# Recurrence levels of a hybrid encoder: keys of both directions in one stationary operand, one matmul per block in place of two

## The reference, cut to what matters

```python
log_f = jnp.logaddexp(jnp.log(lb), jnp.log1p(-lb) + jax.nn.log_sigmoid(z))
k = -jnp.expm1(log_f)
qd = jax.nn.silu(...) * (HG_DK ** -0.5)
...
cum = jnp.cumsum(gc, axis=2)
rel = jnp.where(mask[:, :, None], cum[:, :, :, None, :] - cum[:, :, None, :, :], -jnp.inf)
attn = jnp.einsum('nhtk,nhtsk,nhsk->nhts', qc, jnp.exp(rel), kc)
o = attn @ vc + jnp.einsum('nhtk,nhkv->nhtv', qc * jnp.exp(cum), state)
...
o = o[0] + jnp.flip(o[1], 1)
```

## Time and profile before

| | |
|---|---|
| median of 3 runs | 1437.44 us |
| lowest and highest run | 1436.44, 1437.8 us |
| span of the profiled execution | 1437.8 us |
| time of the profiled execution | 1437.8 us, the highest of the three runs |
| level matmuls, line 767 | 168 instructions, 336 records, from 429.1 us to 531.3 us |
| level 8, line 772 | last starts at 534.18 us |

### The profile page before, as it was taken

The page is one execution under the profiler, slowest core; times in us unless marked ns, Lnnn a source line. Parts: engine busy times, 40 slices in busy tenths (PEclk is TensorE's granted clock), DMA queues, the critical chain, the costliest instruction groups (busy, mean ns, idle before and its releaser), DMA issues.

```text
span 1437.8 us, 23522 instructions
## 1 busy us (share of the span) xinstructions
PE 1329.0 (92%) x9366; PEld 1238.5 (86%) x9366; DVE 1022.9 (71%) x1536; ACT 717.2 (50%) x1147; POOL 150.5 (10%) x122
## 2 busy tenths in 40 slices
PE   7599899999799999799999899899998999699997
PEld 6489799999689998799998798899997998699996
DVE  4186777677859867877778677777678565777677
ACT  4185365555462233555554633655554763555552
POOL 0000300000304430300002002100003001300001
PEclk8789999999999999999999899899998999899999
DMA  7454265555352233365553374455553543265551
GB/s 255 112 202 130 89 202 189 193 190 180 108 183 90 90 103 132 126 227 183 189 186 132 132 231 140 161 205 182 188 188 109 199 133 118 89 233 177 187 191 47
DMA packets 64019, 230.09 MB, mean 160 GB/s; under 512 B 7431, under 2 KB 9223, under 8 KB 62887
## 3 DMA queue, kind: packets, MB, share of 16 engines
q1 hardware_dynamic: 63910, 228.60, 47.6%
HBM read 225.95 MB, written 2.62 MB: 159 GB/s over the span
## 4 chain that ended last, share of the span: by engine, by line
PE 67%; issue 18%; DVE 6%; DMA 4%; POOL 2%; ACT 2%; SPq 0%; POOLq 0%; DVEq 0%; ACTq 0%
PE proj L572 14%; PE proj L573 13%; PE proj L574 13%; PE acc L599 5%; PE acc L601 5%; PE acc L600 5%; DMA raw<-in_stream 4%; PE side L767 2%; PE proj L584 1%; DVE y_tok L1154 1%; PE proj L586 1%; PE proj L588 1%; POOL rstd L1267 1%; DVE w_lo L976 1%; PE acc L668 1%
## 5 line engine op out<-in xcount | busy, mean ns | idle before, releaser
L572 PE MATMUL proj<-xT_hi,w_hi 128*128 128x256 f32 x2000 | 579.8, 290 | 37.5 <-issue 33.0
L976 DVE TENSOR_TENSOR w_lo<-raw,w_hi 128x1024 fp32r<-128x1024 f32 x404 | 480.7, 1220 | 170.2 <-ACT w_hi L784 168.4
L784 ACT ACTIVATE w_hi<-raw 128x1024 fp32r<-128x1024 f32 x404 | 427.1, 1060 | 318.7 <-PE proj L574 144.8
L573 PE MATMUL proj<-xT_lo,w_hi 128*128 128x256 f32 x2000 | 574.2, 287 | 0.0
L574 PE MATMUL proj<-xT_hi,w_lo 128*128 128x256 f32 x2000 | 573.8, 287 | 0.0
L572 PEld LDWEIGHTS proj<-xT_hi,w_hi 128*128 128x128 f32 x2000 | 393.0, 196 | 46.3 <-issue 44.9
L573 PEld LDWEIGHTS proj<-xT_lo,w_hi 128*128 128x128 f32 x2000 | 392.8, 196 | 1.5
L574 PEld LDWEIGHTS proj<-xT_hi,w_lo 128*128 128x128 f32 x2000 | 392.2, 196 | 0.0
L989 DVE SCALAR_TENSOR_TENSOR cv<-hid,fconv_w,cv 128x255 f32<-128x255 f32 x176 | 77.4, 481 | 139.5 <-ACT cv L824 139.5
L601 PE MATMUL acc<-w_hi,gT_lo 128*128 128x512 f32 x352 | 139.0, 395 | 0.0
L600 PE MATMUL acc<-w_lo,gT_hi 128*128 128x512 f32 x352 | 139.0, 395 | 0.0
(11 more groups left out here) (169 smaller groups left out, 1566.1 us busy)
## 6 DMA issues: line engine op xcount, KB each, us to landing
raw<-in_stream SPq DMA_DIRECT2D x404, 512.0 KB, 4.7
gains<-in_ln SPq DMA_DIRECT2D x8, 1024.0 KB, 8.5
bias<-bias_scratch SPq DMA_DIRECT2D x2, 1152.0 KB, 8.0
bias_scratch<-bias_rows SPq DMA_DIRECT2D x1, 1536.0 KB
x_tok<-in_x SPq DMA_DIRECT2D x2, 512.0 KB, 4.4
y_tok<-in_mem SPq DMA_DIRECT2D x1, 1024.0 KB, 10.1
out<-x_tok SPq DMA_DIRECT2D x2, 512.0 KB, 2.8
masks_in<-in_masks_c SPq DMA_DIRECT2D x1, 512.0 KB, 11.5
```

Of the source, the lines that this page charges most:

```text
L572: pe.matmul(bank, w_hi[:, slot, at], a_hi(k, every), start=(k == 0), stop=False)
L573: pe.matmul(bank, w_hi[:, slot, at], a_lo(k, every), start=False, stop=False)
L784: nc.scalar.activation(w_hi[:, u % SPLIT, :], raw[:, u % RAW, :], ACT.Copy).then_inc(hi_ready, 1)
L976: v.tensor_tensor(w_lo[:, u % SPLIT, :], raw[:, u % RAW, :], w_hi[:, u % SPLIT, :].bitcast(F32), ALU.subtract).then_inc(lo_ready, 1)
```

## The change

ScalarE gets a new item "keys" behind each level below 7. It copies, for a pair of heads, the forward keys of the first half and the backward keys of the second half of each double block of the next level, 512 columns, into a free part of the buffer `ex`. TensorE then uses that as the stationary operand and reads the queries crosswise: the first half of each double block from the backward queries, the second half from the forward ones, 128 columns in one matmul. For that `QD` and `KE` become the two halves of one tensor each. The copy waits for the same two grow semaphores as the level's matmuls, which wait for the copy as well.

```diff
@@ make_schedule
                 for n in range(LEVELS + 1):
                     at.setdefault(first + n, []).append(it("level", p, n))
+                    if n + 1 < LEVELS:
+                        at[first + n].append(it("keys", p, n + 1))
@@ trunk_kernel
-        QD = [sb(f"qd{d}", [P, HEADS, SEQ]) for d in range(2)]
-        KE = [sb(f"ke{d}", [P, HEADS, SEQ]) for d in range(2)]
+        qd = sb("qd", [P, 2, HEADS, SEQ])
+        ke = sb("ke", [P, 2, HEADS, SEQ])
+        QD = [qd[:, d] for d in range(2)]
+        KE = [ke[:, d] for d in range(2)]
...
+        def level_keys(p):
+
+            return ex[:].rearrange("p a b c s -> p (a b c s)")[:, p * 512:(p + 1) * 512]
+
+        def crossed(of, lower, p, start, count, b):
+
+
+            other = HEADS * SEQ
+            return bass.AP(tensor=of, offset=lower * other + 2 * p * SEQ + start,
+                           ap=[[2 * other, P], [2 * b, count // (2 * b)], [b + (1 - 2 * lower) * other, 2], [1, b]])
...
+        keys_ready = [sem(f"keys_ready{p}") for p in range(PAIRS)]
@@ tensor, item "level"
+                    if 1 <= n < LEVELS:
+                        pe.wait_ge(keys_ready[p], n)
...
                             elif n < LEVELS:
-
-                                for d in range(2):
-                                    dst = bank[:, col:col + P].rearrange("p (n two b) -> p n two b", two=2, b=b)
-                                    q = QD[d][:, h, keys].rearrange("p (n two b) -> p n two b", two=2, b=b)
-                                    last = pe.matmul(dst[:, :, 1 - d, :], KE[d][:, h, keys], q[:, :, 1 - d, :],
-                                                     start=True, stop=True)
+                                last = pe.matmul(bank[:, col:col + P].rearrange("p (n two b) -> p n two b", two=2, b=b),
+                                                 level_keys(p)[:, col:col + P], crossed(qd, 1, p, col, P, b),
+                                                 start=True, stop=True)
@@ scalar
+                elif name == "keys":
+                    p, n = item[2], item[3]
+                    b = 2 ** (n - 1)
+                    act.wait_ge(fw_ready[p], n)
+                    if n >= 2:
+                        act.wait_ge(bw_ready[p], n - 1)
+                    nc.scalar.activation(level_keys(p).rearrange("p (n two b) -> p n two b", two=2, b=b),
+                                         crossed(ke, 0, p, 0, 512, b), ACT.Copy).then_inc(keys_ready[p], 1)
```

## The result

The changed kernel takes **1445.86 us** (median of 5 runs, 1444.0 to 1446.2) against 1437.5 of the kernel before (5 runs, 1436.44 to 1438.23): ratio 1.0046, 95% interval 1.0031 to 1.0061. It is slower by half a per cent. The forecast was 1438.8, no change, with 1435.9 to 1441.5 as its own range, and the result lies outside that. Only the wider range of 1430 to 1447, which covers the rivals, holds it, and the direction is that of the slower ones.

The account below looks back on a forecast made before the run. TensorE was taken to bound the kernel, VectorE close behind. Schedule -1.6 us plus clock +3.0 gave +1.4 on the 1437.44 median: 1438.8 us, no change, own range 1435.9 to 1441.5, wider range 1430 to 1447.

Parts of the forecast that it names:

- the ring: Layer 1 recurrence levels: the cycle copy, w_hi, w_lo, post work, grow, copy; 5.4 us with FF/FB, 6.8 with HQ.
- Schedule: 105.1 becomes 103.5: Layer 1 recurrence levels, first to last weight load: step sums give 1.6 us won of 18.9.
- Steps with FF/FB post work: Levels 1 to 2 and 3 to 4: 5.50 and 4.84 us before, 5.4 each after.
- Steps without post work: Levels 2 to 3 and 4 to 5, set by GpSimd's chain: 4.85 and 4.65 us before, 4.7 and 4.5 after.
- HQ steps: Levels 5 to 6, with HQ post work on VectorE: 5.49 us before, 6.8 after, TensorE still for 3.1.
- step 7 to 8: Level 8 waits for two grows and two masked copies on VectorE: 7.81 to about 8.2 us; pair two 7.2 after.
- Pair three: Last head pair's levels, V and G chunks with little VectorE work: 26.82 us before, 23.9 after.
- The clock: Slow TensorE clock after four pauses over 2.15 us: 4 by 0.75 = 3.0 us lost, bounds 0 and 6.8.
- Rival 1: Faster: only the copy's 0.60 us and GpSimd's chain hold TensorE; 6 us won, 1431, at best 1426; chance 0.20.
- Rival 2: Slower: ScalarE's gathered two-tensor copy takes 1.0 us, adding 6 us: 1445, up to 1449 with clock loss; chance 0.20.
- Rival 3: At b = 1 (three levels) copy and crossed queries jump at every element and read slowly: +3 us, 1442; chance 0.07.
- Rival 4: The 128-column crossed matmul takes as long as two of 64; levels stay 1.79 us, copies on top, 1447; chance 0.03.

Follow-up runs that it names:

- the clock filled up: The changed kernel with unused-result matmuls in TensorE's pauses before levels 4, 6 and 8, ahead of the side-bank wait: 1446.15 us, ratio 1.0043.

## Why the prediction was right and wrong

**Right: the ring, its members and that it eats the saving.** The prediction named copy, w_hi, w_lo, post, grow as what would stand in the way, and that ScalarE's 50% of idle would not help. The runs show it in both directions: copies that nobody reads cost all of it (1.0042 against 0.9930), and moving the copies behind the next w_hi gives more than half of it back (0.9978). The profile after has the rows named in advance: half the level records, 0.89 us a level, w_hi directly behind the copy, VectorE idle on w_hi.

**Wrong: the size of the ring.** The failed step is "Schedule: 105.1 becomes 103.5". With 3.0 us for the clock the stretch was put at 106.5, and it measured 112.4. Some 3.8 us of it are what the slow clock adds to single steps (below). Without them the schedule is 5.1 us over its 103.5, most of it in two terms.
- *Steps with FF/FB post work*, put at 5.4 us: 6.27 (1 to 2) and 6.15 (3 to 4), and 6.14 in pair two, 2.4 us in all. The post work was taken from a row in which GpSimd was still for the first half (1.49 us). Held back by the ring it runs into GpSimd's grow from its start: 2.30 us, 442.53 to 444.83.
- *Steps without post work*, priced by GpSimd's chain at 4.7 and 4.5 us: 5.38 (2 to 3), and 4.74 (4 to 5 of pair two, at full clock). I let VectorE's work lie beside GpSimd's at no cost. VectorE's grow starts late, at 437.15, and takes 2.5 us to its masked copy instead of the 0.93 of the earlier trace rows. GpSimd's three take 3.0 instead of 2.59 of the earlier trace rows, all of it in the first product, which now runs beside w_lo. (That GpSimd's last operation is shorter at every further level was misread too: the trace before has 0.47, 0.49, 0.32, 0.57, 0.22 and 0.27 us.)

```profile
442.53 0.83 DVE L1052 TENSOR_SCALAR ke<-sig,one_lb 128x256 f32<-128x256 f32 x1
443.28 0.82 DVE L1053 TENSOR_SCALAR tot<-sig,one_lb,lb 128x256 f32<-128x256 f32 x1
...
444.83 0.41 DVE L977 TENSOR_TENSOR qd<-qd,tot 128x256 f32<-128x256 f32 x1
```

The rows ahead of the prediction had both prices: the earlier trace rows at 462.87 shows a first product of 0.84 us with GpSimd beside it and at 453.32 one of 0.46 almost without. I took the free one for operations that the ring itself makes late. HQ steps, put at 6.8, came at 6.16 and 6.69; step 7 to 8 at 8.42 for 8.2 and at 6.69 for 7.2. Pair three was to fall to 23.9 and fell to 25.05. Two smaller slips: the steps of pair one add up to 45.3, not 45.4, and "nothing later gives or takes" missed the 1.4 us that come back behind the last level.

**The clock**, charged with 3.0 us. The trace has slow stretches behind pauses, 0.89 from 429 to 505 in place of 1.00, as forecast from the earlier trace rows. Not every pause of that length has one: behind 2.33 us ahead of level 4 of pair one the step has a granted clock of 0.67, behind 2.32 us ahead of level 4 of pair two 1.00. In single steps the slow clock shows 1.65 us (7.38 against 5.73) and 1.05 and 1.07 (6 to 7, put at 5.0, measured 6.16 and 6.19, with a full clock 5.11 and 5.12). A fourth stretch, 4 to 5 of pair one (5.26 against 4.74 in pair two), is made up in the next step. That is 3.8 us for 3.0 charged. But with the clock filled up the kernel is not measurably faster (1.0043 and 1.0046). So the charge is not borne out as a part of the sum; the schedule was short by more.

**The rivals.** Rival 1, a looser ring, is out for the changed kernel. Its lower figure, 11 us won if copies cost nothing, is close to what the run without copies gives (10 us). Rival 2 gave the right side by the wrong price: its time of 1445 is that measured, its copy of 1.0 us is 0.63. Rival 3, single elements, has its mechanism and not its price: the first copy of a pair (b = 1) takes 0.88 us, the second (b = 2) 0.68, the others 0.63, and the crossed level takes 1.30 us at b = 1, 1.02 at b = 2 and 0.97 above. That is 0.25 + 0.33 us for each of three pairs at most, 1.7 us in all, with part of it hidden. The copy's first row, then min/median/max ns of the copies in the changed kernel and in the one whose copies read one tensor straight:

```profile
423.75 0.88 ACT L952 ACTIVATE ex<-ke 128x512 f32<-128x512 f32 x1 [0.77 <-DVE ksum L1065]
...
L952 ACT ACTIVATE ex<-ke x21: 629/632/875, 423.8 to 535.5; 128x512 f32<-128x512 f32 x21
...
L950 ACT ACTIVATE ex<-ksum x21: 614/630/635, 423.4 to 534.5; 128x512 f32<-128x512 f32 x21
```

The Trainium skill's rule on SBUF cachelines (SBUF — State Buffer, the note under "Door 1: The DMA port swizzle") sets runs of one fp32 apart from runs of two; by it only b = 1 pays. The trace agrees nearly: 0.33 us more a level at b = 1, 0.05 at b = 2. Rival 4 is out: 128 crossed columns take 0.97 us a level.

**The chances.** Slower had 0.34, against 0.44 for no change. That the stated range holds the result is luck as far as the sum goes: it is as wide as the rivals made it, and the mechanism of the one that names 1445 is not the one that acted. The two misses of the schedule have one root: durations measured while the other engine was still or doing something else, used for a schedule in which it is not.

## What to carry to other kernels

An instruction that waits costs what stands behind it in its queue, however idle the engine is. Before adding one, write down the next instructions of that queue and who waits for them, and put it behind the ones that others need: here the place of 21 copies, ahead of the next w_hi or behind it, was the difference between 0.46% slower and 0.22% faster. And when a chain moves work later in time, price that work by rows in which the neighbour that it will now meet is busy, not by rows in which it is still.

## What the runs showed of the hardware that was not expected

- VectorE's products of two SBUF operands and GpSimd's slow each other, to about the sum where both run throughout: the grow's first two products are 0.41 us each with GpSimd still (433.10 in the changed kernel) and 1.08 each with GpSimd beside them (437.15), and GpSimd's product beside them takes 1.03, where its shortest in that trace is 0.62.
- VectorE's w_lo, which reads two SBUF operands too, holds GpSimd up and is not held up itself where it starts first: 12 first products of GpSimd that begin in the first half of a w_lo take 1.26 to 1.44 us, the others 0.78 to 1.10, and w_lo keeps its 1.23 us (1.21 before).
- ScalarE reads two tensors crosswise at full rate in runs of 4 and more: 0.63 us for 512 columns, as the copy that reads one tensor straight. In runs of 2 it takes 0.68, element by element 0.88. TensorE's crossed moving operand behaves alike: 0.97, 1.02 and 1.30 us for 8 records of 128 columns.
